# One block for the peer query of half a and the convolution of half b, the first norm in its block too, and step sizes in four column groups

## The reference

```
h = RMSNorm(x);  z, xBC, dt, q, kv..., gates = split(h @ w_in)
xBC = silu(causal depthwise conv(xBC, 4 taps) + conv_b)
dt  = softplus(dt + dt_bias)           # one step size per token and head (32 heads)
y_ssm  = Mamba-2 SSD(xBC, dt, a_log, d_skip), gated by z, normed
y_attn = native sparse attention(q, kv...)
x += (sigmoid(g1) * y_ssm @ w_ssm_branch + sigmoid(g2) * y_attn @ w_attn_branch) @ w_out
x += PEER(RMSNorm(x))                  # 8 heads, top 16 of 128 x 128 experts each
y  = RMSNorm(x)
```

## Time and profile before

| | |
|---|---|
| median of 3 runs | 2738.09 us (2734.89 to 2739.93) |
| the profiled execution, its own time | 2729.72 us |
| its span in the trace | 2728.0 us |
| busy: TensorE, VectorE, GpSimd, ScalarE | 2018.3, 1465.7, 1467.0, 663.9 us |
| DMA | 843.33 MB, 309 GB/s on average |
| granted TensorE clock, mean over the span | 0.862 of full |

### The profile page before, as it was taken

One profiled execution on the slowest core, in us unless ns is written; L12 is line 12 of the kernel. 1 busy time (PEld: TensorE's weight loads), 2 busy tenths in 40 slices (PEclk: granted clock), 3 DMA queues, 4 the chain that ended last, 5 costly groups with the idle time before them and its releaser, 6 DMA issues. The chain is left out here.

```text
span 2728.0 us, 31363 instructions
## 1 busy us (share of the span) xinstructions
PE 2018.3 (74%) x10891; PEld 1271.3 (47%) x10891; DVE 1465.7 (54%) x3522; ACT 663.9 (24%) x1977; POOL 1467.0 (54%) x1487
## 2 busy tenths in 40 slices
PE   7999989887977979989988946655267776644054
PEld 6778865665645657654444723332144442111011
DVE  3431023236898974457631668878776665106900
ACT  5441026223645220015531113321011110000000
POOL 1110000015457765656654778777867777557774
PEclk9899989988987989989989967876588987878577
DMA  5424454444886899889889879999999999999998
GB/s 181 169 78 139 142 182 158 156 155 165 306 329 216 339 391 396 324 339 335 330 333 401 326 264 382 412 393 337 387 352 411 411 410 385 401 390 409 410 409 312
DMA packets 209781, 843.33 MB, mean 309 GB/s; under 512 B 25752, under 2 KB 32728, under 8 KB 190104
## 3 DMA queue, kind: packets, MB, share of 16 engines
q0 software_dynamic: 170912, 644.95, 61.9%
q1 hardware_dynamic: 38712, 196.36, 19.4%
HBM read 821.80 MB, written 23.54 MB: 310 GB/s over the span
## 5 line engine op out<-in xcount | busy, mean ns | idle before, releaser
L3638 POOL DMA_INDIRECT e_ring<-in_peer_u,e_idx x523 | 620.6, 1187 | 301.4 <-DVE e_dot L3802 142.2
L3802 DVE CUSTOM_DVE_ANT_0 e_ring<-e_ring,e_h 128x1024 f32<-128x1024 f32 x523 | 633.4, 1246 | 66.2 <-PEq L1193 22.0
L3638 POOL DMA_INDIRECT e_ring<-in_peer_v,e_idxT x487 | 505.6, 1038 | 257.7 <-issue 133.0
L3705 PE MATMUL ps<-e_ring,e_wz 128*32 128x512 f32 x1948 | 320.8, 709 | 268.2 <-DMA e_ring<-in_peer_v,e_idxT 159.0
L3705 PEld LDWEIGHTS ps<-e_ring,e_wz 128*32 128x32 f32 x1948 | 67.5, 121 | 425.8 <-issue 421.8
L369 PE MATMUL ps<-hT_ahead,wb 128*128 128x320 f32 x384 | 111.1, 444 | 0.7 <-DMA wb<-in_weights 0.7
L369 PEld LDWEIGHTS ps<-hT_ahead,wb 128*128 128x128 f32 x384 | 73.0, 195 | 30.2 <-issue 3.2
L1849 POOL CAST ra_atf<-ra_at 128x32 f32<-128x32 uint32 x8 | 1.7, 214 | 152.6 <-DVE ra_hit L1842 152.6
L3846 DVE TENSOR_TENSOR e_x<-e_x,ps 128x512 f32<-128x512 f32 x10 | 6.4, 683 | 143.1 <-PE ps L3705 143.1
L1217 POOL MEMSET inda<- 128x256 f32 x1 | 0.3, 312 | 147.7 <-POOLq L4105 147.7
L3705 PE MATMUL ps<-ring_pair,e_wz 128*32 128x512 f32 x152 | 64.2, 736 | 20.6 <-DMA e_ring<-in_peer_v,e_idxT 11.3
(11 more groups left out here) (789 smaller groups left out, 4578.8 us busy)
## 6 DMA issues: line engine op xcount, KB each, us to landing
wb<-in_weights SPq DMA_DIRECT2D x65, 1024.0 KB, 7.3
e_ring<-in_weights SPq DMA_DIRECT2D x36, 1024.0 KB, 4.9
wb<-in_late_weights SPq DMA_DIRECT2D x6, 2048.0 KB, 10.8
room<-in_late_weights SPq DMA_DIRECT2D x6, 2048.0 KB, 16.4
h<-in_weights SPq DMA_DIRECT2D x10, 1024.0 KB, 8.8
xs<-in_weights SPq DMA_DIRECT2D x9, 1024.0 KB, 8.0
e_ring<-in_peer_u,e_idx POOLq DMA_INDIRECT x523, 8.7
e_ring<-in_peer_v,e_idxT POOLq DMA_INDIRECT x487, 11.3
```

What stands on the lines that cost most here:

```text
L3638: nc.gpsimd.indirect_dma_start(out=self.room(place), out_offset=None, in_=k.peer_u if kind == "u" else k.peer_v, in_offset=off).then_inc(s ...
L3705: last = nc.tensor.matmul(k.ps[32 * b:32 * b + 32, self.SUMS + i, :], self.wz[:, at:at + 32], self.room(self.v_at[n])[:, 512 * i:512 * i + ...
L3802: v.tensor_tensor_reduce(uu, uu, self.h[:, tile % 2, :], 1.0, 0.0, ALU.mult, ALU.add, self.dot[:, tile % 2, t:t + 1]).then_inc(self.dotted, 1)
```

## The change

One block is opened ahead of the norm of half a and holds norm, conv, ssd, zgate and branch of half a. Another is opened ahead of the query of half a and holds it and conv, ssd, zgate and branch of half b; the clearing block between them is gone. The semaphores of a stage in a shared block live as long as the block (links). The query of half b keeps its own block.

What the block's end had ordered is now said by waits. TensorE's step matmuls wait for the last spread of the norm, or of Ahead; its first transposes of half b wait until the scores are copied out of banks 2 and 3; SyncE loads the old convolution state once Ahead's tiles are turned. The end of the query of half a on ScalarE (Exp, the waits for shares and names, staging) becomes a function, end_routes, that is called in the convolution of half b at f = 1, between the second fill and the first activation, with waits for the score stores; it stays in place for half b. The selector k.sel is made earlier in GpSimd's list.

The step sizes are computed in four column groups: input block kk goes to rows 32 * (kk % 4) of bank 5, so four partial sums of two blocks each come out in 128 rows. ScalarE copies 128 rows for 32. turn_steps adds the four parts as it transposes: for each token tile four matmuls with the copied rows as stationary and 32 columns of the identity as moving operand.

```diff
-def stage_norm(nc, k, g):
+def stage_norm(nc, k, g, links, block):
+        k.norm_done = (evacuated, NT)
@@ stage_conv, sync
             if g.sample:
+                sp.wait_ge(*k.query_done["ahead_turned"])
                 sp.dma_start(before.rearrange("p f b t -> p (f b t)"), k.conv_before).then_inc(state_in, 16)
@@ stage_conv, tensor
+                if f == 0 and not g.first:
+                    pe.wait_ge(*k.query_done["scores_copied"])
             def project_steps():
+                pe.wait_ge(*(k.norm_done if g.first else k.query_done["ahead_spread"]))
                 pe.wait_ge(*k.w.here(0))
                 for kk in range(KD):
-                    last = nc.tensor.matmul(k.ps[0:HEADS, 5, 0:N], wdt[:, kk, :], k.hT[:, kk, 0:N], start=(kk == 0),
-                                            stop=(kk == KD - 1))
+                    p0 = HEADS * (kk % SPLIT)
+                    last = nc.tensor.matmul(k.ps[p0:p0 + HEADS, 5, 0:N], wdt[:, kk, :], k.hT[:, kk, 0:N], start=(kk < SPLIT),
+                                            stop=(kk >= KD - SPLIT), skip_group_check=True)
             def turn_steps():
-                    last = nc.tensor.transpose(k.ps[0:rows(t), 5, c:c + HEADS], steps_by_head[:, g.cols(t)],
-                                               k.ident[0:HEADS, 0:HEADS])
+                    for q in range(SPLIT):
+                        last = nc.tensor.matmul(k.ps[0:rows(t), 5, c:c + HEADS], steps_by_part[:, g.cols(t)],
+                                                k.ident[:, HEADS * q:HEADS * q + HEADS], start=(q == 0),
+                                                stop=(q == SPLIT - 1))
@@ stage_conv, scalar
-                a.copy(steps_by_head, k.ps[0:HEADS, 5, 0:N]).then_inc(steps_copied, 1)
+                a.copy(steps_by_part, k.ps[:, 5, 0:N]).then_inc(steps_copied, 1)
                 if f < F:
                     fill(f)
+                if f == 1 and not g.first:
+                    k.end_routes()
+                    for scores_out in k.query_done["scores_out"]:
+                        act.wait_ge(*scores_out)
                 if 1 <= f <= F:
                     activate(f - 1)
@@ stage_query, scalar
+            def end_routes():
+                act.wait_ge(shifted, 1)
+                a.activation(k.best[:], k.best[:], ACT.Exp).then_inc(exped, 1)
+                act.wait_ge(routed, 1)
+                act.wait_ge(named, PH)
+                ex.stage_routes(t0)
+            if following:
+                k.end_routes = end_routes
+            else:
+                end_routes()
+                act.wait_ge(ex.staged, t0 + 1)
@@ build
-                        stage_norm(nc, k, g)
+                        links, blocks = ExitStack(), ExitStack()
+                        block = blocks.enter_context(nc.Block(no_gpsimd_drain=True))
+                        stage_norm(nc, k, g, links, block)
-                        with nc.Block(no_gpsimd_drain=True) as block:
+                        blocks.close()
+                        links.close()
-                    stage_query(nc, k, g, second if g.first else None)
-                    clear_semaphores(nc)
+                    links, blocks = ExitStack(), ExitStack()
+                    block = blocks.enter_context(nc.Block(no_gpsimd_drain=True))
+                    stage_query(nc, k, g, second if g.first else None, links, block)
+                    if not g.first:
+                        blocks.close()
+                        links.close()
+                        clear_semaphores(nc)
```

More of the change, by code:

```diff
@@ L137, in stage_norm @@
         k.w.enter(0)
-        block = ctx.enter_context(nc.Block(no_gpsimd_drain=True))
+        k.norm_done = (evacuated, NT)
         @block.sync
@@ L187, in _ @@
             own(gp.tensor_scalar(k.later_s[:], k.cum_s[:], -NEG, NEG, ALU.mult, ALU.add))
+            own(gp.tensor_tensor(k.sel[:], k.identb[:, 0:HEADS], k.identb[:, HEADS:2 * HEADS], ALU.add))
+            own(gp.tensor_tensor(k.sel[:], k.sel[:], k.identb[:, 2 * HEADS:3 * HEADS], ALU.add))
             own(gp.iota(part[:], pattern=[[0, 1]], base=0, channel_multiplier=1))
@@ L321, in stage_conv @@
                              "summed", "negated"))
-        steps_by_head = k.Bs[0:HEADS, 0:N]
+        SPLIT = P // HEADS
+        steps_by_part = k.Bs[:, 0:N]
         dt, da = k.dt[:, t0:t0 + NT, :], k.da[:, t0:t0 + NT, :]
@@ L1929, in spread, with stage_query @@
         last.then_inc(self.evacuated, 1)
-def stage_query(nc, k, g, following):
+def stage_query(nc, k, g, following, links, block):
     with ExitStack() as ctx:
         sb = lambda n, s, d=F32: ctx.enter_context(nc.sbuf_tensor(f"r{g.name}_{n}", s, d))
-        sem = lambda n: ctx.enter_context(nc.semaphore(f"r{g.name}_{n}"))
+        sem = lambda n: links.enter_context(nc.semaphore(f"r{g.name}_{n}"))
         HC, NS_BUF = 2 * PH, 4
@@ L1952, in stage_query @@
         k.w.enter(HC // 2, lambda i: (projected, 2 * i + 2))
-        ahead = Ahead(nc, k, ctx, following) if following else None
-        block = ctx.enter_context(nc.Block(no_gpsimd_drain=True))
+        ahead = Ahead(nc, k, ctx, links, following) if following else None
         @block.sync
@@ L2096, in stage_query @@
         if following:
+            k.query_done = dict(ahead_turned=(ahead.turned, len(following.tiles)),
+                                ahead_spread=(ahead.evacuated, len(following.tiles)), scores_copied=(s_copied, HC),
+                                scores_out=[(out, 16 * (HC // NS_BUF)) for out in s_out])
             k.w.start(following)
@@ L4049, in build @@
                     if g.first:
-                        stage_norm(nc, k, g)
+                        links, blocks = ExitStack(), ExitStack()
+                        block = blocks.enter_context(nc.Block(no_gpsimd_drain=True))
+                        stage_norm(nc, k, g, links, block)
                     with ExitStack() as ssm:
                         allocate_ssm(nc, k, ssm, g)
-                        with nc.Block(no_gpsimd_drain=True) as block:
[L4054 to L4057, removed]
-                                         k.Bnat[:, 0, :].rearrange("p (a n) -> p a n", a=2), block)
+                        stage_conv(nc, k, g, block)
+                        stage_ssd(nc, k, g, block)
+                        stage_zgate(nc, k, g, block)
+                        stage_branch(nc, k, "bs", g, 16, lambda f: k.xnat[:, :, P * f:P * f + P],
+                                     k.Bnat[:, 0, :].rearrange("p (a n) -> p a n", a=2), block)
+                        blocks.close()
+                        links.close()
                     clear_semaphores(nc)
```

14 lines of the change are left out of this document (3 added, 11 removed).

## The result

Over 12 runs each, the changed kernel takes 2713.22 us (2700.55 to 2727.99) and the kernel before 2728.77 (2723.06 to 2739.93). The ratio is 0.9947, 95% interval 0.9925 to 0.9968: 14.5 us faster (8.7 to 20.5); the medians themselves lie 15.6 apart. Two more comparisons of the same two kernels gave 0.9943 (0.9917 to 0.9969) and 0.9952 (0.9933 to 0.9970). The forecast time, 2727.1, lies 13.9 us above the measured median, and the range, which began at 2720, misses it.

What follows compares the result with a forecast made beforehand. Expert gathers were taken to set the end, with TensorE standing still at two seams before it. Gains of 3.0 and 8.0 us sum to 11.0; 2738.1 less 11.0 gives 2727.1 us, range 2720 to 2738.

Steps and rivals of the forecast that it cites:

- The gain, 11.0: Whole kernel: 3.0 us from the norm and convolution of half a plus 8.0 from the query and convolution of half b.
- Seam one: Norm to convolution of half a: steps start at 16.0 instead of 17.45, four column groups shorten them; gain 3.0 us.
- two side effects: Half a: earlier selector on GpSimd, and weight pieces no longer held on SyncE (projection 0's up to 2 us late); costed at nothing.
- Seam two: Query to convolution of half b: steps start at 651.45 instead of 664.05, VectorE then waits for Exp behind fill 1; gain 8.0 us.
- TensorE's larger lead: Half b: projection 1 at 661.0 instead of 675.89, a lead claimed to be thrown away.
- The price of the turning: Turning the steps, both halves: 0.10 us per 32-column instruction by the rows, 1.6 and 2.0 us; 0.025 each by the skill page.
- Lost in the gathers: Rival: in the gather-bound last 1140 us an earlier start just queues longer; 2738 us, chance 0.13.
- Groups don't overlap: Rival: column groups don't overlap, so steps still take 5.25 and 7.1 us; gain 4.5, time 2733.6 us, chance 0.06.
- More passes through: Rival: the end of the routes is not the limit in half b, so TensorE's 14.9 us count; 2720.2 us, chance 0.08.
- Slower: Rival: TensorE stays at half rate until projection 1 ends, both halves; convolutions 4.6 and 1.8 us late; 2744.5 us, chance 0.07.
- the idle that an Exp ends: Sign: VectorE's idle ahead of its first convolution in half b ends by its share, which waited for an Exp behind the second fill.
- the stretches bound by gathers are as long as before: Sign: stretches behind 1588 keep their length; growth there would show the prediction wrong.

Runs made afterwards that it cites:

- best version: Changed kernel with the routes' Exp ahead of half b's first fill and the turning behind projection 1: 2704.13 us, ratio 0.9900 to the kernel before; again 2708.74, 0.9925.

## Why the prediction was right or wrong

**The baseline: wrong, and the largest term.** The forecast set the gain of 11.0 against 2738.09, the median of three runs, though the profiled execution was 8.4 below it. In five comparisons the median of before lay at 2728.8, 2730.9, 2727.9, 2729.1 and 2731.4. The three runs were high by 7 to 10 us. The step of the prediction that failed is the last of its sum, 2738.1 as the median of before: it measured 2728.8. "The median of runs +/- 3" is the bound that failed with it: single runs of this kernel lie between 2713.7 and 2753.4, and three of them don't hold their median to 3. This is 9.3 of the 13.9 us. Against 2728.8 the same sum gives 2717.8, and the forecast's own stretch, 2721 to 2733, becomes 2712 to 2724 and holds the measured 2713.2. The better value was in hand: from the profiled execution, 2729.72, the prediction itself worked out 2718.7 before it turned to the median of three.

**The gain, 11.0: too small as it came out, within what was measured.** The first comparison gave 15.6 between medians and 8.7 to 20.5 as the interval. By the traces: 12.4 us at dt_bias (13.6, 13.0 and 10.6 against the profile shown; one of the two other traces of before lies 1.6 below it). In the means of three traces it is 11.9 us. The last 4.6 us of the miss are not resolved by these runs.

**Seam one, 3.0: inside its bounds of 1.0 to 3.5 in two traces of three, for a reason half seen.** Projection 2 came 1.8, 4.0 and 1.9 us earlier than in the profile shown. The steps start where forecast (15.7 for 16.0), four groups take 1.9 us at half rate (1.7 forecast), turning 1.7 (1.6). The mis-sized term is projection 0, 5.6 us in the first trace for 4.3 forecast: the full rate, which I had fixed at 3.4 us after the start, came 6.0 and 5.7 us after it in the first and third trace. In the second the steps ran in 1.07 us at full rate, and the clock fell behind them; that trace's 4.0 is luck. The two side effects that the prediction cost at nothing cost nothing here: in the rows above TensorE does not idle from the steps to projection 1. Behind this seam, half a's own scatter can hide its gain by 640.

**Seam two, 8.0: right.** The distance fell by 8.3, 7.9 and 7.8, and the chain was the forecast one: Exp behind fill 1, VectorE behind Exp. Its terms: steps 2.2 (2.15), projection 0 5.1 (5.4), turning 2.4 (2.0), projection 1 to fill 4.6 (4.6), fill 1.45 (1.45), Exp to the last share 1.2 (1.45; the last share took 0.29 us where it took 0.55 in the earlier trace rows). Turning is the term that was off: the sixteen instructions of full width took 0.11 us each (1.79) and the eight of the 64-row tile 0.07, for 0.10 and 0.055. That TensorE's larger lead is thrown away was right too: Exp moved forward gets much of it back (distance 28.1, and 25.3 with the turning moved too).

**The price of the turning.** The turning instructions cost 0.106 us each in half a (1.70 for 16) and 0.099 on average in half b (2.37 for 24), so the rows priced them nearly rightly. By the Trainium skill, "TensorEngine Tiling (Array Packing)", section Instruction Overhead, the estimate was 0.025; the traces do not agree: this form, behind a load of 128 columns, costs four times that.

**The rivals.** *Lost in the gathers* fell in its full form: 42.7 us put in came out as 41.8 (31 to 49), and 17 us taken off the distance (best version, with the first seam besides) as a median 20 to 24 under that of before. A loss of a quarter is not excluded. *Groups don't overlap* fell: 16 instructions in 2.2 us where 6.6 are taken in one group. *More passes through* needs the further edits of the best version; this change does not do it. *Slower* did not come: the clock was back after 3.6 to 4.3 us in half b.

**The signs.** Right: the start of the steps, their length, the idle that an Exp ends. Roughly right: the shift from stage to stage, 12 to 16 us and not 11 throughout. Wrong: "the stretches bound by gathers are as long as before" in the one trace that I would have read; its last stretch was 9 us longer, by ten gathers issued at double length.

## What to carry to other kernels

When a block's end is taken away, follow each engine's queue through what is now behind what: here a call that used to be free in the seam's shadow was placed behind a fill and held VectorE for 10.8 us, and moving the call alone took some 6.5 us more off the distance at no price that these runs show. Compare stages by the distance between two marks that bracket the edit, and put the sum against a median of ten or more runs: three runs of this kernel missed their own median by 9 us. Column groups speed up only the instructions that use them; here 2.7 of the 4.4 us that they saved at half rate were paid back, by the next projection and above all by joining the parts. Where gathers set the end, look at the length of each issue too: a row of long issues can starve the queue though its busy share stays near full.

## What the runs showed of the hardware

The granted clock comes back at different moments behind the same work. At the merge of half a, TensorE starts at 503.13 in the kernel before and at 500.13 in the changed one, with the same instructions behind an idle of about 3 us. The kernel before:

```profile
503.00:506.00 3.00, 2.87 (x7) 2.37 (x8) 0.00 (x0) 2.91 (x7) 0.00 (x0) 0.50 1.03 429
506.00:509.00 3.00, 3.00 (x9) 2.37 (x8) 0.00 (x0) 0.94 (x4) 0.00 (x0) 0.50 1.00 421
```

The changed kernel:

```profile
500.00:503.00 3.00, 2.87 (x7) 2.37 (x8) 0.00 (x0) 2.91 (x7) 0.00 (x0) 0.51 1.01 423
503.00:506.00 3.00, 3.00 (x16) 2.64 (x15) 0.65 (x2) 0.93 (x4) 0.00 (x0) 1.00 1.01 426
```

Half rate (1.2 GHz) lasts 6 us in one and 3 in the other, worth 1.5 us, and half a has several such places. They make a scatter of about 3 us at 640, in a kernel against itself (641.6 to 644.5) and between kernels (638.6 to 644.3 with the change or its variants). The traces bear this out: from projection 2 to Ahead's first turn the one with the least time at half rate (47.8 us) takes 609.6 us, the one with the most (61.4) 615.4. "TensorE: Matmul & The Clock Gate", Part 1, of the Trainium skill says that the count of slow matmuls at a start varies from run to run of the same kernel; these traces agree. At the second seam the full rate came 3.6, 4.3 and 4.3 us after the start in the three traces of the changed kernel, and 5.4, 4.8 and 5.5 in those of the kernel before.

In the gather-bound end the transfers run at 409 GB/s in most executions and at 371 to 381 over some 110 us in others. The DMA share of 0.99 for 1.03 hides that the queue ran short: ten or eleven gathers in a row were issued in 1.98 us instead of 0.97, 2.29 us apart, while VectorE ran its dots 1.15 us apart without a pause. It costs some 9 us (242.9 to 246.9 from the last ranking to the end, against 234.3 to 237.9) and was seen in four traces of fourteen, with either kernel. Rows of up to seven long issues cost nothing that the traces show. What starts the long rows stays open.
